# How the second expert matrix is cut into load chunks, in a one-core mixer and mixture-of-experts kernel

## The reference, cut to what matters

```
logits = x @ w_router + b_router;  top 4 of 32 experts, softmax over the 4
for each expert e, over the tokens that chose it:
    hid = x @ w1[e] + b1[e]                      # 1024 -> 2048
    glu = min(hid[:, :1024], 7);  lin = clip(hid[:, 1024:], -7, 7)
    act = glu * sigmoid(1.702 * glu) * (lin + 1) # 1024 columns
    y  += weight * (act @ w2[e] + b2[e])         # 1024 -> 1024, sum over 1024 rows of w2
```

## Time and profile before

| | |
|---|---|
| median of 3 runs | 1835.25 us (1834.8 to 1836.32) |
| span of the profiled execution, first to last instruction | 1833.9 us |
| PE busy | 1796.6 us (98% of the span) |
| DVE / ACT / POOL busy | 462.5 / 263.1 / 343.1 us |
| moved by DMA | 486.00 MB, mean 265 GB/s |

### The profile page before, as it was taken

How to read it: one execution, slowest core, us unless ns; L and a number is a source line. 1 busy time by engine, 2 the same in 40 slices (tenths; PEclk the granted TensorE clock), 3 DMA queues, 4 the chain that set the end, 5 groups by cost and what they waited for, 6 DMA issues and landing times.

```text
span 1833.9 us, 37414 instructions
## 1 busy us (share of the span) xinstructions
PE 1796.6 (98%) x15909; PEld 872.7 (48%) x15909; DVE 462.5 (25%) x936; ACT 263.1 (14%) x562; POOL 343.1 (19%) x383
## 2 busy tenths in 40 slices
PE   7999999999999999899999999999999999999996
PEld 5676666555454445344444444444444444444434
DVE  4455455443341015401001010010110100101103
ACT  2320221221120011110011100100111001011001
POOL 2011010001005002411321312213123122131212
PEclk9999999999999999899999999999999999999998
DMA  6222212112015251699999999999999999999995
GB/s 200 72 69 68 70 49 72 35 49 55 23 46 178 69 204 37 249 407 407 401 399 408 394 407 406 394 407 398 402 408 393 406 405 396 408 395 406 407 395 206
DMA packets 156153, 486.00 MB, mean 265 GB/s; under 512 B 15569, under 2 KB 81009, under 8 KB 123297
## 3 DMA queue, kind: packets, MB, share of 16 engines
q1 hardware_dynamic: 133664, 452.27, 63.1%
q0 software_dynamic: 21232, 32.99, 7.5%
q10 hardware_dynamic: 1216, 0.18, 0.1%
HBM read 465.98 MB, written 19.56 MB: 265 GB/s over the span
## 4 chain that ended last, share of the span: by engine, by line
PE 96%; DVE 2%; ACT 1%; DMA 0%; issue 0%; POOL 0%; SPq 0%; POOLq 0%; ACTq 0%; DVEq 0%
PE PS L1775 36%; PE PS L394 21%; PE PS L1787 18%; PE PS L1589 6%; PE PS L1677 3%; PE PS L1549 2%; PE PS L1632 2%; PE PS L1760 1%; PE PS L1753 1%; PE PS L1768 1%; PE PS L1501 1%; PE PS L1636 1%; PE PS L1622 1%; PE PS L1440 1%; DMA x_sb<-in_x 0%
## 5 line engine op out<-in xcount | busy, mean ns | idle before, releaser
L1775 PE MATMUL PS<-ring,mix_sb 128*32 128x512 f32 x6144 | 672.9, 593 | 0.3 <-issue 0.3
L1775 PEld LDWEIGHTS PS<-ring,mix_sb 128*32 128x32 f32 x6144 | 196.8, 110 | 433.7 <-issue 425.3
L1787 PE MATMUL PS<-ring,hm_sb 128*32 128x256 f32 x6144 | 337.4, 379 | 0.9 <-ACT hm_sb L924 0.9
L1787 PEld LDWEIGHTS PS<-ring,hm_sb 128*32 128x32 f32 x6144 | 199.6, 110 | 146.0 <-issue 18.6
L1387 DVE TENSOR_SCALAR hm_sb<-PS 128x768 f32<-128x768 f32 x32 | 30.6, 957 | 901.3 <-PE PS L1775 901.3
L710 POOL DMA_INDIRECT acc_dram<-hm_sb,ints x93 | 147.1, 1582 | 45.3 <-POOL ints L728 24.7
L394 PE MATMUL PS<-uT_sb,ring 128*128 128x512 f32 (+3 forms) x400 | 141.9, 511 | 0.0
L728 POOL COPY ints<-ints 128x3 int32 (+1 forms) x31 | 5.8, 187 | 710.4 <-ACT hm_sb L935 710.4
L394 PEld LDWEIGHTS PS<-uT_sb,ring 128*128 128x128 f32 x400 | 75.4, 190 | 64.3 <-issue 59.3
L688 POOL DMA_INDIRECT mix_sb<-xt_dram,ints x96 | 94.5, 984 | 56.6 <-POOL ints L717 22.6
L394 PE MATMUL PS<-ring 128*128 128x129 f32 (+3 forms) x472 | 82.9, 333 | 0.6 <-ACT ring L791 0.6
(11 more groups left out here) (296 smaller groups left out, 1386.6 us busy)
## 6 DMA issues: line engine op xcount, KB each, us to landing
ring<-in_w SPq DMA_DIRECT2D x384, 1024.0 KB, 19.6
ring<-in_w_in SPq DMA_DIRECT2D x24, 512.0 KB, 4.1
ring<-in_w_in SPq DMA_DIRECT2D x8, 1024.0 KB, 5.3
ring<-m_dram POOLq DMA_DIRECT2D x16, 256.0 KB, 4.5
ring<-in_w_m_proj SPq DMA_DIRECT2D x8, 512.0 KB, 3.8
ring<-in_w_a_proj SPq DMA_DIRECT2D x8, 512.0 KB, 3.8
ring<-in_w_out SPq DMA_DIRECT2D x1, 4096.0 KB, 15.5
x_sb<-in_x SPq DMA_DIRECT2D x4, 512.0 KB, 7.3
```

The costliest lines, as they stand in the source:

```text
L1775: last = nc.tensor.matmul(PS[32 * j:32 * j + 32, t, :].rearrange("p (c n) -> p c n", c=2), xgT[n][:, k, 32 * t:32 * t + 32], w1_c[k][:, :, ...
L1787: last = nc.tensor.matmul(PS[32 * j:32 * j + 32, 3 + t, 0:QR], actT[:, k, 32 * t:32 * t + 32], w2_c[k // 2][:, k % 2, j * QR:(j + 1) * QR] ...
```

## The change

It has two halves that belong together.

The first is the load of w2. Before, chunk c held rows 256c to 256c + 127 as its first contraction tile and rows 256c + 128 to 256c + 255 as its second, so partition p received row 256c + p and row 256c + 128 + p: two pieces of 4 KB. Now partition p receives rows 256c + 2p and 256c + 2p + 1, which are neighbours in memory: one piece of 8 KB. The first contraction tile of a chunk now holds its even rows, the second its odd rows.

The second half makes the activations agree. In `turn_act` the transpose for h no longer takes columns 128h to 128h + 127 of `act_sb`, but columns h, h + 2, h + 4 and so on, again 128 of them. Partition p of contraction tile 2j + h is then feature 256j + 2p + h. The bytes moved, the number of instructions, every wait and the matmuls of `down` stay as they are.

```diff
-    w2v = w2.rearrange("e (k p) n -> p e k n", p=P)
+    w2v = w2.rearrange("e (j p h) n -> p e j (h n)", j=4, p=P)
...
         def load_w2(c, e):
-            sp.dma_start(w2_c[c], w2v[:, bass.ds(e, 1), 2 * c:2 * c + 2, :].rearrange("p e k n -> p (e k) n")).then_inc(chunk_in[8 + c], 16)
+            sp.dma_start(w2_c[c].rearrange("p k n -> p (k n)"),
+                         w2v[:, bass.ds(e, 1), c, :].rearrange("p e n -> p (e n)")).then_inc(chunk_in[8 + c], 16)
...
                 for t in range(TT):
-                    last = nc.tensor.transpose(PS[:, 6 + h, t * P:(t + 1) * P], act_sb[:, t, h * P:(h + 1) * P], ident)
+                    last = nc.tensor.transpose(PS[:, 6 + h, t * P:(t + 1) * P], act_sb[:, t, :].rearrange("p (c h) -> p h c", h=2)[:, h], ident)
```

## The result

The change made the kernel slightly slower. Over 20 runs each, the median went from 1837.28 us (1834.8 to 1839.34) to 1840.43 us (1838.05 to 1842.75), a ratio of 1.0018 with a 95% interval of 1.0012 to 1.0024. The 1835.25 us shown ahead of the prediction were the median of three runs, 2 us under that of the twenty; the ratio is the number to go by. The ratios and intervals here are those on record; they can differ from the quotient of the two medians by a few units in the last digit.

What follows compares the result with a forecast made beforehand. The prediction took PE to set the pace, with DMA full but not waited for. From 1835.25 us, -0.24 for the expert 1 stall and 0 for the transposes gave 1835.0 us, range 1833.5 to 1838.0 us.

Steps and rivals of the forecast that it cites:

- What bounds the kernel: Routed steps: PE sets the pace at 33.20 us; DMA is full, needs about 33.28 us, and is not waited for.
- The loads of w2: w2 loads in each step: 0.12 us less a chunk, 0.49 us less a step, hidden beneath PE except once.
- cover: Slack of w1 loads: a slot is needed again after 30.6 us, landing takes 20.8 us at worst, leaving 9.8 us.
- The drain: Backlog of w1 loads: landing time of line 498 falls by 0.41 us a step, from about 18.3 to about 7 us.
- the 0.24 us of stall in the step of expert 1: Step of expert 1: 33.44 us becomes 33.20 as its four waits for DMA go, -0.24 us once.
- The transposes: 192 activation transposes on PE's path, now with strided weight loads: 0 to 2.4 us more, 0 taken.
- the upper end: Activation transposes: strided loads at 191 ns, first of a batch 50 ns later, others 5 ns, 2.4 us in all.
- slower, by the load of weights: Rival at the activation transposes: strided loads take three or four times the variable part, 12 or 23 us; middle 1850 us, chance 0.08.
- the forecast's own band of 0.2%: Whole kernel: a difference within 0.2%, 3.7 us, counts as the same time; chance of same 0.87.

Runs made afterwards that it cites:

- both batches strided: The kernel before with every second column read in the transposes of activations and of gathered tokens; 1842.64 us against 1837.35, ratio 1.0027.
- two versions with 8 KB pieces: The change with packed transposes, 1837.76 us against 1838.04; and the change with VectorE sorting even and odd columns, transposes packed, 1837.79 us against 1838.04.
- by turns: The change with a step's two transpose batches merged, packed token and strided activation transposes alternating, packed first; 1839.58 us against 1838.04, ratio 1.0012.
- tokens first: The change with the six packed token transposes placed ahead of the six strided activation transposes; 1839.19 us against 1837.23, ratio 1.0011.
- the shortened work with 8 KB pieces: The kernel before with 8 KB w2 pieces, packed transposes and the third token tile in only two contraction tiles of `down`; 1818.95 us against 1837.35.

## Why the prediction was wrong, step by step

**What bounds the kernel** was right: PE, with DMA full beside it and 0.07 us a step behind. Taking 2.6 us of work from PE laid the DMA pace open where the backlog had put it.

**The loads of w2** were right in kind: off the path, cover intact, nothing gained. The price was off by a third, 0.32 us a step against 0.49. The two windows it was read from are short and do not hold the same mix: in the earlier trace rows q0 works beside q1, in the earlier trace rows it does not. Whether that is the reason was not tried. The drain was 0.37 us a step, near the 0.41 forecast, but that is luck: 0.11 of it is the slower PE, and with packed transposes it was 0.26. The one thing forecast as a gain, the 0.24 us of stall in the step of expert 1, cannot be found. Without a drop of the clock that step took 33.44 us in the profile of before, 34.54 with strided transposes alone, 34.31 with both batches strided and 33.59 with a step of four elements, all with 4 KB pieces, and 34.12 and 33.99 in two versions with 8 KB pieces. It varies by more than was to be won. What sets its length was not found.

**The transposes** are where it failed: "Nearest row above: the load becomes like the plain f32 one, 191 ns", and so 2.4 us as the upper end and 0 as the value taken. The upper end was no bound. A strided load took 208 ns, the first of a batch was late by 58 ns, where 50 were allowed, and each of the other five by 10 ns, where the forecast allowed 5. The forecast had more room there than the kernel has: its 118 ns between two transposes spread the delay of the first over the batch, and the others follow each other at 109 ns. Against that the variable part of the strided load, 208 - 85 = 123 ns, is too long. From which length on a load shows was not measured closely: at 197 ns, by turns, it still cost 8 ns. That makes 0.108 us a step and 3.5 us in all. The choice of 0 rested on nothing but that the nearest row was the packed load; with both ends open, the middle of the range would have been the honest value, and the range needed room above a row that described another operation. By mechanism, what happened is the small end of the rival "slower, by the load of weights" (0.08). It had the right mechanism, but asked for three or four times the variable part where (208 - 85) / 57 = 2.2 times was enough.

**The rule of the Trainium skill** (SBUF — State Buffer, section Door 1) that a read of two hits for each line of 16 bytes keeps full rate does not hold here: at two hits the load went from 141 to 208 ns. Nor does its other half: at one hit it took 211 ns, hardly more. For this operand, the measurement decides.

**The level.** The range was set around 1835.25 us, a median of three runs, and 20 runs gave 1837.28. Even so the forecast ratio of 0.9999 lies outside the measured interval: a gain of 0.24 us was forecast, and 3 us were lost. A loss of 0.18% still counts as no difference by the forecast's own band of 0.2%, but that is owed to the width of the band and not to the mechanism.

## What to carry to other kernels

When a layout is changed so that one side reads better, ask which engine reads the other side with a step, and put the step on an engine that does not set the pace: VectorE took it at the same 481 ns, TensorE's weight load did not. Look at how long a weight load is beside the matmul that hides it: the 208 ns loads here stuck out by 10 ns behind each transpose, with no averaging over shorter neighbours. And the first load of a batch was bare, 57 ns when packed and 58 more when strided, so the packed batch belonged first; the first comes behind matmuls of another tile shape (128*32), but whether the shape is the reason was not tried. And full DMA engines are not a bound by themselves: what tells is whether the landing time grows and who waits; here a change by 0.3 us a step of DMA time was worth nothing until PE had been made 2.6 us faster.

## What was not expected of the hardware

A float32 weight load of 128 columns takes 141 ns packed, and 208, 200 and 211 ns with steps of 8, 12 and 16 bytes: one rise, and then flat. VectorE's two-input product shows no such rise (480 and 481 ns).

TensorE's granted clock fell to 1.2 GHz for about 3.4 us in the step of expert 1 in five of the twelve profiles: after, by turns, tokens first, a step of three elements, and the shortened work with 8 KB pieces. It did not in the other seven, although the wait for VectorE ahead of it was 2.23 or 2.28 us in all of them, and 2.23 us in some on either side. What decides it was not found. At 1.7 us it is as large as half of the effect that was measured here, so a single profile must not be read for a difference of this size; the pitch of 27 steps can.
